# Dilated attention run in quarters of the heads beside the next products, with head gains folded into the turned copies and the rotation tables

## The chip, the cores and the metric

One core of one Trainium2 chip runs the whole program. The metric is the device time of one execution in microseconds (us), as the median of several runs. The engines are TensorE (PE, its weight load is PEld), VectorE (DVE), ScalarE (ACT), GpSimd (POOL) and SyncE (SP, which only issues the loads of weights). Each engine executes its own list of instructions strictly in order and waits on semaphores for the others.

## What is computed

Two blocks of two layers each over 256 tokens of width 1024, in float32. The change touches one sublayer, the dilated attention of layer 1 of the first block:

```python
def dilated_attention(h, cos, sin, w_in, q_gain, k_gain, w_out):
    B, S, _ = h.shape
    H, hd = DIL_HEADS, HEAD_DIM                      # 16 heads of 64
    proj = (h @ w_in).reshape(B, S, N_DIL_GROUPS, 3, H, hd)
    outs, lses = [], []
    for g, (window, dilation) in enumerate(DIL_CONFIGS):      # (128,1) (512,4) (2048,16)
        q = apply_rope(rms_norm(proj[:, :, g, 0], q_gain[g]), cos, sin)
        k = apply_rope(rms_norm(proj[:, :, g, 1], k_gain[g]), cos, sin)
        o, lse = dilated_group(q, k, proj[:, :, g, 2], window, dilation)
        outs.append(o)
        lses.append(lse)
    alpha = jax.nn.softmax(jnp.stack(lses, axis=0), axis=0)
    o = jnp.sum(alpha[..., None] * jnp.stack(outs, axis=0).astype(jnp.float32), axis=0).astype(h.dtype)
    return o.reshape(B, S, H * hd) @ w_out
```

`rms_norm` is taken over the 64 elements of a head, and `apply_rope` turns only the first 16 of them.

## The kernel before, in words

A planner (class `Plan`/`Program`) writes one list of steps; every engine's program then walks that list and emits its own part of each step, so the order of the list is the order on each engine. Weights are read in pieces of 1 MB (four chunks of 128 rows by 512 columns) into six raw buffers. For exact float32 products each piece is converted to a high part on ACT (`whi`, step `conv_hi`) and a low part on DVE (`wlo`, `conv_lo`), into three buffers; a conversion is planned when an earlier piece is taken, and waits for PE to have read the buffer. A product unit (`token`) uses two pieces: 24 matmuls of 512 columns each, high times high, high times low, low times high.

The dilated sublayer takes 18 units: for each half of the heads (8 heads) and each of three groups, q, then k, then v (`dil_in`). After a q or k unit a head norm runs: ACT squares the two result banks, DVE sums per head (`TENSOR_REDUCE dhs`), ACT takes the root, DVE takes the reciprocal, multiplies the banks by it (event `hn_mul`, which also frees the two banks), multiplies by the gain (`dgn`), does six small multiplies with the rotation table (`rope`) and an add (event `hn_out`). PE then turns the result (`head_turn`, eight transposes into banks D0 and D1) and ACT copies it out as `dqT` or `dkT`. In the code before, this turn is planned at the end of the following unit (`run_turns` in `token`).

When a half's nine units are done, `dil_attn` plans its attention in one block with no products between: ten steps, each two heads for one half of the queries. The parts of a step are the scores (PE), the mask and row minimum (DVE, `S,nm<-ps,dmask`, event `biased`), the exponentials (ACT, event `expd`), the reciprocal and its multiply (DVE, event `weighed`), the turn of the weights of the two heads (PE, `ps<-ident,S`), its copy (ACT, `PT`) and the product with v (PE, `ps<-PT,dv`). For even steps a head has 256 columns of scores, for odd ones 512. The second half's block is followed by the out product (`out_units`): four pieces, whose banks for the first two pieces are D0 to D3 before. The output of the first half is kept in `doT` and split into high and low parts just before the second block.

The older forgetting attention of layer 0 already runs its attention beside products: `beside` is a list of closures, and `run_beside` pops one after each part of a piece (`self.parts`).

## Time and profile before

| | us |
|---|---|
| median of 3 runs | 2218.18 (2216.0 to 2218.39) |
| profiled execution, its own time | 2219.53 |
| span of the profiled execution | 2218.2 |
| PE busy | 2140.0 (96%) |
| DVE busy | 1497.4 (68%) |
| ACT busy | 1082.5 (49%) |
| mean granted TensorE clock | 0.988 of full |

PE is the engine that sets the time: it is busy for 96% of the span, and the other engines matter where PE waits for them. A time inside the span is read from its start. The dilated sublayer's products begin at 793.96 and its out product ends at 1090.68.

### The profile page before, as it was taken

Reading aid. Unit: us, or ns where it says so; the run is one execution under the profiler, and the core shown is the slowest. Engines: PE = TensorE matmul, PEld = TensorE weight load, DVE = VectorE, ACT = ScalarE, POOL = GpSimd, SP = SyncE. Lnnn points to the kernel's source line nnn. Section 1 sums busy time; section 2 is a strip of 40 time slices with the busy share of each in tenths; the row PEclk is TensorE's granted clock in tenths of the full one; section 3 lists DMA queues with packets and bytes.
Section 4 is the critical chain, followed back from the end, with each engine's and each line's share of the span. In section 5 each row is a group of like instructions: output and inputs, shape, how many; then the busy total and the mean of one; then the engine's idle time right before and its main releaser. Section 6 shows DMA issues by size and latency. Waiting matters only on the chain.

```text
span 2218.2 us, 33120 instructions
## 1 busy us (share of the span) xinstructions
PE 2140.0 (96%) x14096; PEld 1889.0 (85%) x14096; DVE 1497.4 (68%) x1960; ACT 1082.5 (49%) x1217; POOL 156.6 (7%) x192
## 2 busy tenths in 40 slices
PE   7999998999999999899999999999999999999998
PEld 5998765998899878687799887897998878988996
DVE  4677676877777786576655455568786655677874
ACT  4443565543444354555544346644554457444652
POOL 0311110111011100000000011100000111000000
PEclk9999998999999999999999999999999999999999
DMA  9977662987787855244355564435655564446651
GB/s 347 307 267 263 249 244 86 302 279 271 249 273 257 288 210 182 88 171 152 115 191 189 190 226 169 171 124 166 217 178 194 194 211 153 136 152 209 190 176 53
DMA packets 262818, 448.61 MB, mean 202 GB/s; under 512 B 11616, under 2 KB 147104, under 8 KB 262416
## 3 DMA queue, kind: packets, MB, share of 16 engines
q1 hardware_dynamic: 243616, 376.64, 50.2%
q0 software_dynamic: 18768, 68.75, 8.8%
q8 instruction: 111, 1.82, 0.3%
q10 hardware_dynamic: 288, 1.11, 0.1%
q14 instruction: 35, 0.29, 0.0%
HBM read 445.40 MB, written 1.06 MB: 201 GB/s over the span
## 4 chain that ended last, share of the span: by engine, by line
PE 88%; ACT 5%; DVE 5%; issue 1%; DMA 0%; SPq 0%; ACTq 0%; DVEq 0%
PE ps L1522 86%; ACT whi L1747 2%; DVE wlo L1952 1%; PE ps L1713 1%; PE ps L1680 1%; ACT S L1747 1%; ACT L1747 1%; ACT xhi L1747 1%; ACT xs L1747 0%; DVE S L2100 0%; DMA raw<-in_mod_w 0%; PE ps L1670 0%; DVE nbuf L2060 0%; ACT PT L1747 0%; PE ps L1630 0%
## 5 line engine op out<-in xcount | busy, mean ns | idle before, releaser
L1952 DVE TENSOR_TENSOR wlo<-raw,whi 128x2048 fp32r<-128x2048 f32 (+1 forms) x339 | 767.2, 2271 | 349.8 <-ACT whi L1747 349.3
L1747 ACT ACTIVATE whi<-raw 128x2048 fp32r<-128x2048 f32 (+1 forms) x339 | 640.7, 1895 | 363.6 <-PE ps L1522 343.7
L1522 PE MATMUL ps<-xhi,whi 128*128 128x256 f32 x2632 | 649.8, 287 | 6.4 <-DVE wlo L1952 4.4
L1522 PE MATMUL ps<-xhi,wlo 128*128 128x256 f32 x2632 | 643.5, 284 | 0.0
L1522 PEld LDWEIGHTS ps<-xhi,whi 128*128 128x128 f32 x2632 | 507.9, 193 | 11.7 <-issue 7.2
L1522 PEld LDWEIGHTS ps<-xhi,wlo 128*128 128x128 f32 x2632 | 508.0, 193 | 2.3 <-issue 2.0
L1522 PE MATMUL ps<-xlo,whi 128*128 128x256 f32 x2632 | 344.3, 283 | 0.1
L1522 PEld LDWEIGHTS ps<-xlo,whi 128*128 128x128 f32 x2632 | 327.6, 192 | 0.5 <-DVE xlo L2066 0.3
L1522 PE MATMUL ps<-whi,xhi 128*128 128x512 f32 x736 | 296.7, 403 | 13.5 <-DVE wlo L1952 10.5
L1522 PE MATMUL ps<-wlo,xhi 128*128 128x512 f32 x736 | 290.4, 395 | 0.0
L1522 PE MATMUL ps<-whi,hhi 128*128 128x512 f32 x528 | 210.0, 398 | 0.0
L1522 PE MATMUL ps<-wlo,hhi 128*128 128x512 f32 x528 | 209.8, 397 | 0.0
L1522 PE MATMUL ps<-whi,hlo 128*128 128x512 f32 x528 | 207.9, 394 | 0.0
L1522 PE MATMUL ps<-whi,xlo 128*128 128x512 f32 x736 | 185.7, 391 | 0.0
L1522 PEld LDWEIGHTS ps<-whi,xhi 128*128 128x128 f32 x736 | 140.5, 191 | 48.4 <-issue 11.6
L1522 PEld LDWEIGHTS ps<-wlo,xhi 128*128 128x128 f32 x736 | 140.6, 191 | 27.8 <-issue 0.2
L1522 PEld LDWEIGHTS ps<-whi,xlo 128*128 128x128 f32 x736 | 139.3, 189 | 29.3
L1522 PEld LDWEIGHTS ps<-whi,hhi 128*128 128x128 f32 x528 | 99.2, 188 | 25.1 <-issue 0.7
L1522 PEld LDWEIGHTS ps<-whi,hlo 128*128 128x128 f32 x528 | 99.1, 188 | 23.5
L1522 PEld LDWEIGHTS ps<-wlo,hhi 128*128 128x128 f32 x528 | 99.2, 188 | 23.5 <-issue 0.7
L1747 ACT ACTIVATE e<-ps 128x512 f32<-128x512 f32 (+1 forms) x48 | 30.4, 634 | 172.4 <-PE ps L1522 172.3
L1747 ACT ACTIVATE hhi<-e 128x512 fp32r<-128x512 f32 x66 | 41.7, 632 | 114.0 <-DVE e L2254 71.2
(234 smaller groups left out, 1966.7 us busy)
## 6 DMA issues: line engine op xcount, KB each, us to landing
raw<-in_w_in SPq DMA_DIRECT2D x52, 1024.0 KB, 4.9
raw<-in_ffn_w_gate SPq DMA_DIRECT2D x88, 512.0 KB, 4.6
raw<-in_ffn_w_up SPq DMA_DIRECT2D x88, 512.0 KB, 6.0
raw<-in_ffn_w_down SPq DMA_DIRECT2D x44, 1024.0 KB, 5.0
raw<-in_w_up SPq DMA_DIRECT2D x88, 512.0 KB, 4.8
raw<-in_dil_w_in SPq DMA_DIRECT2D x36, 1024.0 KB, 5.1
xs<-in_mod_w POOLq DMA_DIRECT2D x54, 512.0 KB, 6.2
nbuf<-in_mod_w POOLq DMA_DIRECT2D x46, 512.0 KB, 5.2
```

The costliest lines, as they stand in the source:

```text
L1522: return nc.tensor.matmul(o, lhs, rhs, start=start, stop=stop, skip_group_check=True)
L1680: ins = nc.tensor.transpose(ps[:, D2, h * T + b * P:h * T + (b + 1) * P], w["S"][:, j, b * P:(b + 1) * P], ident[:, :])
L1713: ins = nc.tensor.transpose(ps[:, D0 + c // 2, (c % 2) * T + t * P:(c % 2) * T + (t + 1) * P], tms[s["name"]][:, t, c * P:(c + 1) * P], id ...
L1747: return nc.scalar.activation(o, i, func, **kw)
L1952: V.tensor_tensor(wlo[:, s["c"], 0:s["n"]], raw[:, s["slot"], 0:s["n"]], whi[:, s["c"], 0:s["n"]].bitcast(F32), ALU.subtract).then_inc(sem ...
```

## The change

The attention of the sublayer is made in quarters (4 heads, n = 0 to 3) and taken apart into smaller steps that are placed between halves of product pieces.

- Units: `dil_qk(n, g)` makes q and k of a quarter in one unit (256 columns each), `dil_values_in` makes v of a half. The order is qk 0, v 0, qk 1, qk 2, v 1, qk 3, each for the three groups.
- `self.parts` is two halves of a piece; after each half piece `run_beside` pops one entry. For quarters 0 to 2 the attention is 13 entries: per step p one with scores and exponentials of p and values of p-1, one with the reciprocal and its multiply (`weigh`), one with the turn. `None` entries (7, 0, 6, 0) delay it.
- `turns_early`: a head norm's turn is planned after the first piece of the following unit and no longer at its end.
- Quarter 3's attention (six entries, `last_step`) is placed beside the out product, whose units now use banks G0 to G3; the first two chunks of its second pieces are made early (`early=2`).
- The gain multiply of the head norm is gone for the dilated heads: the gains of the 48 unturned elements are the scale of ACT's copies `dqT` and `dkT` (`dgc`), those of the 16 turned ones are multiplied into the rotation tables once, on POOL (`dil_rope`, tile `drp`). The norm's work tile is now `nbuf`, and its rotation scratch `mrow`.

The diff, cut to its core:

```diff
+            if self.turns_early:
+                self.run_turns()
...
+    def dil_qk(self, n, g):
+
+        if g == 0:
+            self.at = self.dil_heads[n] = []
+        b0, b1, tok = self.token(self.need_x)
+        if (n, g) == (3, 2):
+            for c in range(4):
+                self.split_chunk(c, ("dil", 0), self.o_ready[c])
+        turn = self.head_norm(b0, b1, tok, "dil", g, ("dil", g, n % 2), [self.gain, self.late, self.rope_gain], self.dil_scored[n % 2])
+
+        def begin():
+            turn()
+            self.beside.extend([None] * (7, 0, 6, 0)[n] + self.dil_attention(n))
+
+        if (n, g) == (3, 2):
+            self.beside.extend([None] * 6 + [begin])
...
+        else:
+            self.turns.append(begin if g == 2 else turn)
...
+        def step(p, part):
+            if part == 0 and p < 4 * n + 4:
+                scores(p)
+                exps(p)
+            if part == 0 and p > 4 * n:
+                values(p - 1)
+            if part == 1:
+                weigh(p)
+            if part == 2:
+                turn(p)
+
+        def last_step(p):
+            if p < 16:
+                scores(p)
+            if p > 13:
+                values(p - 2)
+            if 12 < p < 17:
+                turn(p - 1)
+            if p < 16:
+                exps(p)
+                weigh(p)
...
+        pcs = self.last_two()
+        for kk in range(early):
+            for u in range(2):
+                self.token_step(pcs[u], need, src, base + u, base + 2 + u, 4, NC, (kk,), [])
+                self.run_beside()
         while self.beside:
             self.run_beside()
...
-                tail = self.out_units("x", self.need_x, lambda: Tail(self, "gate", "rms", 1, 1))
+                tail = self.out_units("x", self.need_x, lambda: Tail(self, "gate", "rms", i, 1), G0, True, 2 * i)
...
-                    V.tensor_tensor(tv, tv, gain.unsqueeze(1).to_broadcast([P, 16, 64]), ALU.mult).then_inc(sem["hn_out"])
...
+                        act(dq[:, :, :].rearrange("p c (t r i) -> p (c t) r i", t=2, r=2),
+                            ps[:, D0, :].rearrange("p (c i r) -> p c r i", c=4, r=2), ACT.Identity,
+                            scale=dil_gc[:, 0, g:g + 1]).then_inc(sem["head_kept"])
```

How this moves instructions is seen in three places. Line numbers are those of the kernel that the rows belong to. The first is DVE in the attention, before: the mask of two heads is followed at once by their reciprocals and multiplies (`ri<-rs` and `S<-S,ri`).

```order
L2092 ISA S,nm<-ps,dmask 128x256 [waits score]
L2092 ISA nm 128x1
L2092 ISA S,nm<-ps,dmask 128x256
L2092 ISA nm 128x1
L2097 RECIPROCAL ri<-rs 128x1 [waits expd]
L2100 TENSOR_SCALAR S<-S,ri 128x256 [waits weighed]
L2097 RECIPROCAL ri<-rs 128x1 [waits expd]
L2100 TENSOR_SCALAR S<-S,ri 128x256 [waits weighed]
```

In the change the same place for step 2 of quarter 0, after the first qk unit of quarter 1 (n = 1, g = 0). The rows left out are five of the six rotation multiplies and, after the last row, the second head's.

```order
L2169 ISA S,nm<-ps,dmask 128x256 [waits turned,score]
L2169 ISA nm 128x1
L2169 ISA S,nm<-ps,dmask 128x256 [waits turned]
L2169 ISA nm 128x1
L2190 TENSOR_REDUCE dhs<-nbuf 128x16 [waits hn_sq]
L2192 RECIPROCAL dhs<-dhs 128x16 [waits hn_sqrt]
L2195 TENSOR_TENSOR nbuf<-ps,dhs 128x1024 [waits head_turn,hn_rec]
L2206 TENSOR_TENSOR mrow<-nbuf,drp 128x8x16 [waits hn_mul]
...
L2213 TENSOR_TENSOR nbuf<-mrow 128x16x16 [waits ropa]
L2029 TENSOR_TENSOR wlo<-raw,whi 128x2048 [waits w_hi]
L2174 RECIPROCAL ri<-rs 128x1 [waits expd]
L2177 TENSOR_SCALAR S<-S,ri 128x256 [waits weighed]
```

Between the mask and the reciprocal there now stand that unit's whole head norm and the low part of a weight piece.

The second place is PE around the same step: scores (`dkT,dqT`), values of the step before (`PT,dv`), two half pieces of products (left out but for their last row), then the turn of the two heads' weights and the head norm's turn (`ident,nbuf`).

```order
L1588 MATMUL ps<-dkT,dqT 128x128 [waits biased,pt]
L1588 MATMUL ps<-dkT,dqT 128x128
L1588 MATMUL ps<-dkT,dqT 64x64 x8
L1588 MATMUL ps<-PT,dv 64x128 x4
L1588 MATMUL ps<-PT,dv 64x64 x8
...
L1588 MATMUL ps<-whi,xlo 128x512 x4
L1736 MATMUL ps<-ident,S 128x128 [waits weighed]
L1736 MATMUL ps<-ident,S 128x128
L1736 MATMUL ps<-ident,S 128x128 [waits biased,weighed]
L1736 MATMUL ps<-ident,S 128x128
L1780 MATMUL ps<-ident,nbuf 128x128 [waits biased,pt,hn_out]
L1780 MATMUL ps<-ident,nbuf 128x128 x7
```

The turn is two half pieces behind the scores, and waits for `weighed`, which DVE reaches only after the rows above.

The third place is PE where the last product unit (n = 3, g = 2) ends and the out product begins.

```order
L1588 MATMUL ps<-wlo,xhi 128x512
L1588 MATMUL ps<-whi,xlo 128x512 x4
L1588 MATMUL ps<-whi,xhi 128x512 [waits split_hi,w_lo,hn_mul]
L1588 MATMUL ps<-wlo,xhi 128x512
L1588 MATMUL ps<-whi,xhi 128x512
L1588 MATMUL ps<-wlo,xhi 128x512
L1588 MATMUL ps<-whi,xlo 128x512 [waits split_lo]
```

The out product's first matmul waits for `hn_mul`, the multiply of the last head norm: its banks G0 and G1 are those of the last unit. In the code before the last unit was a v unit and the block of attention stood in between.

On ACT, 56 table loads before are 68 after: the root of a head norm and the exponentials use different tables, and they now alternate.

## Rows read from the trace of the kernel before

**Rows 1.** The page: busy time, share of the span and instructions of each engine.
```profile
PE 2140.0 (96%) x14096; PEld 1889.0 (85%) x14096; DVE 1497.4 (68%) x1960; ACT 1082.5 (49%) x1217; POOL 156.6 (7%) x192
```
**Rows 2.** Busy time by stretch: A:B length, PE, PEld, DVE, ACT, POOL, clock, DMA share, GB/s.
```profile
898.96:931.42 32.46, 25.50 (x355) 18.69 (x353) 17.46 (x65) 22.23 (x55) 0.00 (x0) 0.89 0.17 62
931.42:1035.47 104.05, 104.05 (x483) 86.60 (x480) 72.11 (x84) 50.84 (x40) 0.00 (x0) 1.00 0.47 163
1035.47:1068.69 33.22, 24.95 (x354) 18.48 (x352) 19.73 (x72) 23.54 (x59) 0.00 (x0) 0.90 0.18 61
```
**Rows 3.** Busy time by stretch: one pair of attention steps, and the slow start.
```profile
904.70:910.20 5.50, 5.36 (x44) 4.02 (x44) 3.69 (x15) 2.91 (x8) 0.00 (x0) 0.54 0.00 1
913.20:919.40 6.20, 5.62 (x94) 4.16 (x88) 3.71 (x15) 4.47 (x13) 0.00 (x0) 1.00 0.00 0
```
**Rows 4.** Timeline of PE: one piece of products, then a head turn.
```profile
845.82 0.39 PE L1522 MATMUL ps<-whi,xhi 128*128 128x512 f32 x1
...
851.26 1.03 PE L1713 MATMUL ps<-ident,S 128*128 128x128 f32 x8
852.05 0.48 PE L1522 MATMUL ps<-whi,xhi 128*128 128x512 f32 x1
```
**Rows 5.** Timeline of ACT and DVE: one head norm (the rotation multiplies left out).
```profile
853.25 1.02 ACT L1747 ACTIVATE S<-ps 128x1024 f32<-128x1024 f32 x1
...
856.19 1.23 DVE L2119 TENSOR_TENSOR S<-ps,dhs 128x1024 f32<-128x1024 f32 x1
857.45 1.23 DVE L2121 TENSOR_TENSOR S<-S,dgn 128x1024 f32<-128x1024 f32 x1
...
859.78 0.43 DVE L2136 TENSOR_TENSOR S<-PT 128x256 f32<-128x256 f32 x1
```
**Rows 6.** Groups by line and shape, 899 to 932: xcount, busy us, mean ns.
```profile
L1747 ACT ACTIVATE S<-S,nm 128x512 f32<-128x512 f32 x8 | 5.7, 715 | 0.2 <-DVE nm L2092 0.2
L2092 DVE CUSTOM_DVE_ANT_0 S<-ps,dmask 128x512 f32<-128x512 f32 x8 | 5.2, 687 | 0.3 <-PE ps L1522 0.3
L1747 ACT ACTIVATE S<-S,nm 128x256 f32<-128x256 f32 x8 | 4.0, 501 | 0.0
L2100 DVE TENSOR_SCALAR S<-S,ri 128x512 f32<-128x512 f32 x8 | 3.9, 487 | 0.3
L1747 ACT ACTIVATION_READ_ACCUMULATOR S<-S,nm 128x1 f32 x16 | 3.1, 192 | 0.0
L2092 DVE CUSTOM_DVE_ANT_0 S<-ps,dmask 128x256 f32<-128x256 f32 x8 | 3.1, 420 | 1.8 <-PE ps L1522 1.8
L1747 ACT ACTIVATE PT<-ps 128x256 f32<-128x256 f32 x8 | 3.0, 377 | 0.6 <-PE ps L1670 0.6
L2100 DVE TENSOR_SCALAR S<-S,ri 128x256 f32<-128x256 f32 x8 | 2.8, 354 | 0.3
L2097 DVE RECIPROCAL ri<-rs 128x1 f32<-128x1 f32 x16 | 2.6, 164 | 9.8 <-ACT S L1747 9.8
```
**Rows 7.** Groups by line and shape, 832 to 900: the conversions of a weight piece.
```profile
L1952 DVE TENSOR_TENSOR wlo<-raw,whi 128x2048 fp32r<-128x2048 f32 x12 | 27.1, 2287 | 9.7 <-ACT whi L1747 9.7
L1747 ACT ACTIVATE whi<-raw 128x2048 fp32r<-128x2048 f32 x12 | 22.9, 1910 | 5.3 <-PE ps L1522 5.3
```
**Rows 8.** Timeline of PE after idle times; the idle time stands in brackets.
```profile
1042.66 1.18 PE L1670 MATMUL ps<-ident,S 128*128 128x128 f32 x4 [3.82 <-DVE S L2100]
...
1095.57 1.35 PE L1630 MATMUL ps<-ident,xs 128*128 128x128 f32 x8 [1.94 <-DVE xs L2029]
...
792.64 1.09 PE L1630 MATMUL ps<-ident,xs 128*128 128x128 f32 x8 [1.77 <-DVE xs L2029]
```
**Rows 9.** Timeline of ACT: the split of four kept chunks.
```profile
1038.77 1.33 ACT L1747 ACTIVATE xhi<-doT 128x256 fp32r<-128x256 f32 x4
```
**Rows 10.** Timeline of ACT: the switch to the root's table after the first block.
```profile
943.68 1.28 ACT L1747 ACT_TABLE_LOAD   x1
944.98 0.31 ACT L1747 ACTIVATE dhs<-dhs,epst 128x16 f32<-128x16 f32 x1
```

More of the change, by code:

```diff
@@ L199, in run_beside @@
     def run_beside(self):
-        if self.beside:
-            self.beside.pop(0)()
+        step = self.beside.pop(0) if self.beside else None
+        if step:
+            step()
     def next_pair(self):
@@ new lines, in scores, with biased @@
+    def scores(self, name, c, p, n, banks, ready):
+        tok = self.ev("pe", "score")
+        self.add("scores", name=name, c=c, qt=p % 2, kl=n, banks=banks, bank_free=[self.free[b] for b in banks], ready=ready)
+        return tok
+    def biased(self, name, j, n, bank, score, ready=None):
+        tok = self.ev("dve", "biased")
+        self.add("bias", name=name, j=j, n=n, bank=bank, score=score, s_free=self.s_free[j % 4], ready=ready)
+        self.free[bank] = self.bias_done = tok
+        return tok
@@ new lines, in exps, with weigh, values @@
+    def exps(self, name, j, n, after):
+        tok = self.ev("act", "expd")
+        self.add("exp", name=name, j=j, n=n, biased=after)
+        return tok
+    def weigh(self, name, j, n, after):
+        tr, td = self.ev("dve", "weighed"), self.ev("dve", "weighed")
+        self.add("weigh", name=name, j=j, n=n, expd=after, recip=tr)
+        return td
+    def values(self, name, c, hd, p, kl, pt, ready):
+        tok = self.ev("pe", "value")
+        self.add("values", name=name, hd=hd, qt=p % 2, kl=kl, bank=D3, bank_free=self.free[D3] if p % 2 == 0 else None, pt=pt, ready=ready)
+        self.pt_free[0] = self.pt_free[1] = tok
+        return tok
@@ L583, in turn_pair, with attention @@
+    def attention(self, name, klen, ready, emit, bias_ready=None, after=None):
+        rec = []
+        def scores(p):
+            n = klen(p % 2)
+            tok = self.scores(name, p // 2, p, n, (D0, D1), ready[:-1] if p == 0 else [])
+            for w in range(2):
+                rec.append([self.biased(name, 2 * p + w, n, D0 + w, tok, bias_ready(2 * (p // 2) + w) if bias_ready else None), n])
         def turn_pair(p):
@@ L591, in turn_pair @@
                 rec[j].append(te)
-        def values(p):
-            c, qt = p // 2, p % 2
-            bank = D3 if compact else G2 + c % 2
-            kl = rec[2 * p][2]
-            tok = self.ev("pe", "value")
-            self.add("values", name=name, p=p, kl=kl, bank=bank, bank_free=self.free[bank] if qt == 0 else None,
-                     pt=[rec[2 * p][3], rec[2 * p + 1][3]], ready=ready[-1])
-            self.pt_free[0] = self.pt_free[1] = tok
-            if qt == 1:
-                emit(c, bank, tok)
         def step_of(p):
@@ L664, in head_norm, with head_turn @@
         self.free[b0] = self.free[b1] = t4
-        out = t7 if turned else t5
-        self.turns.append(lambda: self.head_turn(name, out, dst, 1.0))
-    def head_turn(self, name, after, dst, scale):
+        at = self.at
+        return lambda: self.head_turn(name, out, dst, 1.0, at, gain_ready, dst_free)
+    def head_turn(self, name, after, dst, scale, at, gain_ready=(), dst_free=None):
         tk = self.ev("pe", "head_turn")
-        te = self.ev("act", "head_kept")
-        self.add("head_turn", name=name, after=after, dst=dst, scale=scale, bank_free=[self.free[D0], self.free[D1]], head_turn=tk)
-        self.free[D0] = self.free[D1] = te
+        te = [self.ev("act", "head_kept") for _ in range(2 if name == "dil" else 1)]
+        self.add("head_turn", name=name, after=after, dst=dst, scale=scale, bank_free=[self.free[D0], self.free[D1]], head_turn=tk,
+                 gain_ready=gain_ready, dst_free=dst_free)
+        self.free[D0], self.free[D1] = te[0], te[-1]
@@ L813, in fox_in @@
         if r < 2:
-            self.head_norm(b0, b1, tok, "fox", r, ("fox", "qk"[r], hh), gain_ready=[self.gain, self.late])
+            self.turns.append(self.head_norm(b0, b1, tok, "fox", r, ("fox", "qk"[r], hh), [self.gain, self.late]))
         else:
@@ L835, in dil_begin @@
         self.late = self.late_loads("dil_loads", 3)
+        self.parts, self.turns_early = (range(0, 2), range(2, 4)), True
+        self.o_ready = [None] * 6
+        self.dil_heads = {}
+        self.dil_scored = [None] * 2
+        self.dil_v, self.dil_valued = [], None
+        self.dil_keep = self.emit_keep(("dil", 0), self.o_ready)
+        self.dil_split = self.emit_split("dil", "x", 6, self.x_split)
     def dil_gain(self):
         self.gain = self.ev("dve", "gain")
-        self.add("dil_gain", late=self.late)
```

313 lines of the change are left out of this document (158 added, 155 removed).

## The prediction, made before the changed kernel ran

> **What bounds the kernel now.** The page comes first: PE is busy for 96% of the span [rows 1], so a change counts by the time in which PE waits or runs slowly. Next the busy time by stretch. In a stretch of products alone PE is busy for all of 104.05 us at a granted clock of 1.00, though DVE and ACT have only 72 and 51 us to do there. The two blocks of attention last 32.46 and 33.22 us with PE busy for about 25, part of it at a lower clock [rows 2]. Those two blocks are what the change can win. In the middle of a block two steps repeat every 6.2 us with 5.62 us of PE's work at full clock [rows 3]. Eight such pairs are 45.0 us, so of the 65.7 us in the blocks **20.7 us** are waits and slow clock. Were all attention covered by products, the time would fall by just that.
>
> The prices of the parts follow. A weight piece takes PE 5.44 us and a head turn with its aftermath about 0.9 [rows 4]. A head norm runs from the square's start at 853.25 to the end of `hn_mul` at 857.42, which is 4.17 us, and on to the end of its add at 860.21. Without the gain multiply of 1.23 that is 5.7 us from square to add [rows 5]. A pair of masks is 0.8 us (256 columns) or 1.35 (512), a first exponential with its read 0.65 or 0.85, a pair 1.15 or 1.65, a reciprocal and multiply 0.55 or 0.68 each, a pair of copies of turned weights 0.65 [rows 6]. A conversion is 1.9 us on ACT, then 2.25 on DVE at the pitch of a pair [rows 7].
>
> **The change, part by part.**
>
> *Removed:* both blocks, 20.7 us as above. The twelve gain multiplies, 14.7 us of DVE, shorten the norms as counted. Nothing else on PE goes away; its matmuls and turns stay as many.
>
> *Added at no cost:* twelve more table loads on ACT of 1.28 us. The load before a root lies beside the sum on DVE, and the root starts 1.30 us after the load did [rows 10]; the load before an exponential lies beside the scores. If that cover goes, each is 1.3 us on its chain. The Trainium skill, page ScalarE: Activation LUTs, section What ACT_TABLE_LOAD costs, has a switch cost 2.66 us with a drain of 1.38 behind the load. No drain shows in the row. By the page's 1.38, as an estimate, five chains would bring some 7 us more. Twenty-four more loads on SP, with half as long rows, in a stretch where the DMA engines are busy for 0.47 of the time [rows 2]: no cost, and if they came late, the conversions would. POOL's two table products need some us at the start, before the first norm's multiply; nothing.
>
> *(a) Early head turns.* A turn is now one piece, 5.44 us, behind its unit, and the norm needs 5.7 after the unit. Where no attention lies between (four units: n=0 and the last of n=1) PE waits 0.3 us each, **1.2 us**.
>
> *(b) A mask at a unit's end.* The main term. DVE works in order, and step 2 of quarter 0 has its mask before, and its reciprocal behind, the norm of the unit just ended. From the end of the scores: first mask and two exponentials 1.55, copy of an output 0.4, norm 5.7, low part 2.25, two reciprocals and multiplies 1.05, semaphores 0.3, in all 11.2 us until the second head may turn. PE has the values (1.05) and two half pieces (5.44) to do, and the first head's turn (0.3): 6.8. It waits about 4.2 us, and the head norm's turn then waits 0.4 for the copy that frees bank D0: 4.6. Before it, step 0's mask falls before a conversion: exponentials 1.55, 1.9, 2.25, weighing 1.1, less 5.44 and 0.3, is another 1.2. Quarter 2 has the same pattern: 2 x 5.8 = **11.6 us**.
>
> *(c) Quarter 1* is laid one half piece later. Its first norm ends, with a low part and both masks of step 5 behind it on DVE, 9.95 us after the unit; PE, with 5.44 of products, the turn, scores and values in 7.85, waits 2.1 for the bank, then 0.7 for step 5's weighing. The next norm holds up step 6's mask for 1.9. Step 7 is a case (b) with 512 columns: 2.35 + 5.7 + 2.25 + 1.35 and semaphores, less what PE has (0.6 + 5.44 + 0.65), 4.9 and 0.6 for the bank. Together **10.2 us**.
>
> *(d) The end.* The out product may not start before the last norm's `hn_mul`: four splits on ACT of 1.33 [rows 9], then 4.17 [rows 5], plus a semaphore: 5.6. Nothing else stands in PE's queue. Its seven chunks hide the rest of that norm. The six last steps have one chunk (1.36 us) between them, against a chain of mask, exponentials and weighing of 3 to 4 us with a conversion in the midst: I count 2.5 us at step 14's scores, 0.5 at step 15's turn and 0.7 at its values. Together **9.3 us**.
>
> *(e) Clock.* After 3.82 us idle PE is granted half speed for a while; after 1.94 too, after 1.77 not [rows 8]. Of the price: 904.7 to 910.2 is such a time, at 0.54 [rows 3], and does in 5.4 us what takes 3.4 at full clock, so 2.05 us. Four waits are clearly long enough: (b) twice, step 7 and the out product: **8.2 us**. Three near 2 us could add up to 6; with none the term is 0.
>
> The sum: 1.2 + 11.6 + 10.2 + 9.3 + 8.2 = 40.5 added, 20.7 removed, net **+19.8 us**. On the profiled execution's 2219.5 us that is 2239.3; the median of the runs shown is 1.35 us lower, so **2238.0 us**. Bounds: without term (e) 2229.8, with three more slow times 2244, a few us more if small switches cost more. The forecast's own range is 2229 to 2247.
>
> **Rivals.**
>
> *The waits of (b) and (c) do not come* (faster). The mechanism: reciprocal and multiply reach DVE within the 6.8 us that PE has to do, so the turns find their rows ready and all of quarters 0 to 2 is hidden. Then only (a), (d) and one slow time stay: 2218.2 - 20.7 + 1.2 + 9.3 + 2.05 = 2210. It decides at 11.2 against 6.8 us: 4.4 us would have to vanish from a chain of measured parts in an order that is fixed. For it: the stretch of products shows both engines with a third of their time free. Against: the order of rows on DVE. Chance 0.10.
>
> *The waits absorb one another* (no change). If PE's wait in one unit gives DVE and ACT the lead for the next, (b) and (c) could come to half, and the clock be lost twice: 1.2 + 10.9 + 9.3 + 4.1 - 20.7 = +5, and with (d) shorter about 2220. I followed the lead through in (c) and it was gone each time by the next norm. Chance 0.08.
>
> *The waits come, but not the slow clock* (slower, less): 2230, by the 1.77 us row. Chance 0.15.
>
> *The table switches cost time on the chain* (slower, more). If each root started a load's length (1.28 us) later than counted, five chains of (b) and (c) would be that much longer: 2238 + 6 = 2244. The gap of 1.30 us between load and root speaks against it [rows 10]. Chance 0.05. The drain in the page of the Trainium skill named above would act in this way.
>
> That the change does not do what it says can be left out: the order shows the attention between the pieces.
>
> **How the numbers follow.** The forecast has 0.62. Every case but the first two is slower by more than 0.2% (4.4 us, about what a measurement of this kernel can tell from no change): 0.82. No change 0.08, faster 0.10. The range from 2222 to 2248 leaves out the faster case, part of the second, and a few hundredths above.
>
> **What would show it.** In the changed profile: PE waiting about 4 us for `S` of DVE in two places, about 5 in a third, at turns of weights (`ident,S`); about 5.6 us before the first out product, released by DVE's `hn_mul`; waits of about 2 us at head turns in quarter 1; the clock near one half behind each long wait; the sublayer from 793.96 to 1090.68 longer by some 20 us, other stages unchanged. Wrong would be turns without waits, or a sublayer shorter than 290 us.

## The result, and the profile after

The changed kernel takes **2248.95 us** (median of 4 runs, 2245.12 to 2250.83) against 2218.05 for the kernel before (4 runs). The ratio is 1.0141, with a 95% interval of 1.0129 to 1.0154: slower by 31 us. The forecast was 2238 us in a range of 2222 to 2248, so the sign was right, the size too small by a third, and the time lies 1 us above the range.

The page's busy times of the changed kernel, which answer to [rows 1]:

```profile
PE 2144.9 (96%) x14096; PEld 1885.6 (84%) x14096; DVE 1483.7 (66%) x1948; ACT 1101.6 (49%) x1243; POOL 158.1 (7%) x194
```

DVE has 13.7 us less to do, about the twelve multiplies that went, ACT 19 more, and PE is as busy as before in its share: the page alone would not show what became slower. The busy times by stretch do (columns as in [rows 2]). First the changed kernel: all before the sublayer, the sublayer, the stretch from its last product to the next stage's first, and the rest.

```profile
0.00:789.32 789.32, 750.47 (x5029) 657.28 (x5029) 561.05 (x734) 360.08 (x413) 107.89 (x152) 0.99 0.77 262
789.32:1111.17 321.85, 291.28 (x1762) 229.65 (x1762) 187.05 (x319) 176.28 (x234) 2.57 (x5) 0.96 0.41 137
1111.17:1120.51 9.34, 4.57 (x34) 2.90 (x33) 4.90 (x12) 5.54 (x12) 0.00 (x0) 0.87 0.76 253
1120.51:2243.80 1123.29, 1098.54 (x7276) 995.78 (x7274) 730.67 (x885) 559.72 (x587) 47.62 (x38) 0.99 0.52 174
```

The same four stretches of the kernel before:

```profile
0.00:793.96 793.96, 757.71 (x5028) 664.13 (x5029) 561.14 (x734) 359.90 (x413) 107.64 (x152) 0.98 0.76 260
793.96:1090.68 296.72, 281.48 (x1762) 228.59 (x1762) 202.28 (x335) 159.90 (x211) 1.24 (x3) 0.98 0.42 149
1090.68:1096.96 6.28, 4.30 (x34) 2.26 (x33) 3.19 (x8) 3.01 (x9) 0.00 (x0) 0.94 0.63 208
1096.96:2218.20 1121.24, 1096.52 (x7274) 994.07 (x7274) 730.78 (x885) 559.70 (x587) 47.69 (x38) 0.99 0.52 175
```

The sublayer is 25.1 us longer, the stretch behind it 3.1, and the rest 2.1; the part before it is 4.6 shorter. To split a sublayer's length further, I take PE's idle time (length less busy time), the time that slow clock cost (busy time multiplied by one less the granted clock, summed over windows of 1 us), and what remains, PE's work at full clock:

| sublayer | length | idle | slow clock | work at full clock |
|---|---|---|---|---|
| before | 296.72 | 15.2 | 6.3 | 275.2 |
| changed | 321.85 | 30.6 | 11.9 | 279.4 |

Idle time and slow clock together rise by 21.0 us, where the forecast had 19.8. Work at full clock rises by 4.2 us although no matmul was added, and the stretch behind grows by 3.1: these two the forecast did not have. The part before the sublayer, in which both kernels do the same work (DVE x734, ACT x413 and POOL x152 in both rows), is discussed with the verdict.

Here are PE's waits of 0.25 us or more in the changed sublayer and at its end, in order of time (the idle time and its releaser in brackets; `ident,nbuf` is a head turn, `ident,S` a turn of attention weights; rows that repeat one shown are left out).

```profile
808.29 1.09 PE L1780 MATMUL ps<-ident,nbuf 128*128 128x128 f32 x8 [1.46 <-DVE nbuf L2213]
...
863.44 0.90 PE L1736 MATMUL ps<-ident,S 128*128 128x128 f32 x4 [0.48 <-DVE S L2177]
889.24 1.15 PE L1736 MATMUL ps<-ident,S 128*128 128x128 f32 x4 [3.51 <-DVE S L2177]
890.91 1.94 PE L1780 MATMUL ps<-ident,nbuf 128*128 128x128 f32 x8 [0.52 <-issue]
...
937.27 1.06 PE L1780 MATMUL ps<-ident,nbuf 128*128 128x128 f32 x8 [1.76 <-DVE nm L2169]
944.42 1.25 PE L1736 MATMUL ps<-ident,S 128*128 128x128 f32 x8 [0.62 <-DVE S L2177]
954.95 1.06 PE L1780 MATMUL ps<-ident,nbuf 128*128 128x128 f32 x8 [1.72 <-DVE nm L2169]
973.97 1.64 PE L1736 MATMUL ps<-ident,S 128*128 128x128 f32 x8 [4.51 <-DVE S L2177]
976.35 1.94 PE L1780 MATMUL ps<-ident,nbuf 128*128 128x128 f32 x8 [0.73 <-issue]
...
1068.35 0.80 PE L1588 MATMUL ps<-whi,xhi 128*128 128x512 f32 x1 [5.53 <-DVE nbuf L2195]
1090.28 0.41 PE L1736 MATMUL ps<-ident,S 128*128 128x128 f32 x2 [3.33 <-DVE nm L2169]
1104.34 1.12 PE L1588 MATMUL ps<-PT,dv 128*64 128x128 f32 x24 [0.78 <-ACT PT L1814]
1118.89 1.97 PE L1696 MATMUL ps<-ident,xs 128*128 128x128 f32 x8 [4.77 <-DVE xs L2106]
```

The last row is the wait that stood at 1.94 before (1095.57, [rows 8]). Of the others, all but one are in places that the prediction named. The one is the wait of 3.33 us: the prediction had 2.5 us at step 14's scores and 0.5 at step 15's turn, and PE waited at neither. It waited at the turn of step 12's second head, whose bank D0 comes free with step 13's mask, and on DVE that mask stood behind a low part:

```profile
1087.23 2.29 DVE L2029 TENSOR_TENSOR wlo<-raw,whi 128x2048 fp32r<-128x2048 f32 x1 [1.25 <-ACT whi L1814]
1089.44 0.68 DVE L2169 CUSTOM_DVE_ANT_0 S<-ps,dmask 128x512 f32<-128x512 f32 x1
```

DVE around the wait of 3.51 (the reciprocal, the rotation multiplies and the add left out):

```profile
879.42 0.42 DVE L2169 CUSTOM_DVE_ANT_0 S<-ps,dmask 128x256 f32<-128x256 f32 x1
...
881.86 1.22 DVE L2190 TENSOR_REDUCE dhs<-nbuf 128x16 f32<-128x1024 f32 x1 [2.00 <-ACT nbuf L1814]
...
883.76 1.23 DVE L2195 TENSOR_TENSOR nbuf<-ps,dhs 128x1024 f32<-128x1024 f32 x1
...
886.43 2.28 DVE L2029 TENSOR_TENSOR wlo<-raw,whi 128x2048 fp32r<-128x2048 f32 x1
888.63 0.16 DVE L2174 RECIPROCAL ri<-rs 128x1 f32<-128x1 f32 x1
```

ACT had finished both exponentials, with their reads, at 880.64. The reciprocal that PE waited for came 8.0 us later, behind 2.0 us in which DVE itself waited for the square, and behind the norm and the low part.

ACT in the same place, where the changed table is loaded beside DVE's sum:

```profile
881.84 1.28 ACT L1814 ACT_TABLE_LOAD   x1
883.13 0.31 ACT L1814 ACTIVATE dhs<-dhs,epst 128x16 f32<-128x16 f32 x1
```

The load ends with the sum (883.08) and the root starts 1.29 us after the load did: the switch costs nothing here, as the prediction had it.

### The profile page after: what moved, and what is told of

Same layout as the page of the kernel before. It is cut to its first block, busy times and chain, and to the rows that moved or that the text cites. A ratio compares the mean times of both kernels' runs of the same rounds, so it can differ in the third digit from the quotient of the medians.

```text
span 2243.8 us, 33163 instructions
## 1 busy us (share of the span) xinstructions
PE 2144.9 (96%) x14096; PEld 1885.6 (84%) x14096; DVE 1483.7 (66%) x1948; ACT 1101.6 (49%) x1243; POOL 158.1 (7%) x194
## 3 DMA queue, kind: packets, MB, share of 16 engines
HBM read 445.30 MB, written 1.06 MB: 199 GB/s over the span
## 4 chain that ended last, share of the span: by engine, by line
PE 80%; DVE 9%; ACT 6%; DMA 2%; issue 2%; SPq 0%; ACTq 0%; DVEq 0%
PE ps L1588 78%; DVE wlo L2029 3%; ACT whi L1814 2%; DMA xs<-in_mod_w 1%; DMA raw<-in_ffn_w_up 1%; PE ps L1780 1%; ACT L1814 1%; ACT S L1814 1%; DVE nbuf L2195 1%; PE ps L1746 1%; PE ps L1736 1%; DVE nbuf L2137 1%; ACT xhi L1814 1%; ACT xs L1814 0%; ACT nbuf L1814 0%
## 5 line engine op out<-in xcount | busy, mean ns | idle before, releaser
L1588 PE MATMUL ps<-whi,xhi 128*128 128x512 f32 x736 | 302.6, 411 | 19.1 <-DVE wlo L2029 10.5
L1588 PE MATMUL ps<-whi,xlo 128*128 128x512 f32 x736 | 194.3, 392 | 0.0
L1588 PEld LDWEIGHTS ps<-whi,hhi 128*128 128x128 f32 x528 | 99.2, 188 | 25.1 <-issue 0.7
```

Source lines behind the costliest of these rows:

```text
L1588: return nc.tensor.matmul(o, lhs, rhs, start=start, stop=stop, skip_group_check=True)
```

## The experiments

Twelve kernels were run, each against the kernel before on the same chip. They come in the order in which they ran. The kernel before took 2217.56 us beside the first four, 2217.34 beside the next four and 2219.34 beside the last four (16, 27 and 16 runs), so kernels of different groups are compared by their ratios to it and by their profiles. "The sublayer" is measured as in the table above.

### One step group moved: q0_shift

```diff
+            steps = self.dil_attention(n)
+            if n == 0:
+                steps = steps[:6] + [None] * 3 + steps[6:9] + [None] + steps[9:]
-            self.beside.extend([None] * (7, 0, 6, 0)[n] + self.dil_attention(n))
+            self.beside.extend([None] * (7, 0, 6, 0)[n] + steps)
```

> The changed kernel with one difference: in quarter 0 three empty entries stand ahead of step 2 and one ahead of step 3, so both masks are planned at the third half piece of a unit and their weighing at the fourth, ahead of the unit's head norm on VectorE; the last values still come before quarter 1 begins. Theory A (term (b): the wait comes from VectorE's order, mask before and reciprocal behind the norm): the waits of 3.51 and 0.52 us at step 2 of quarter 0 go, and with them the half-speed stretch behind them (some 2 us); head turns without attention near them cost 0.35 each as elsewhere. Quarter 2, left as it was, keeps its 3.50 and 0.52. About 6 us less than the change: 2243. Rival B (VectorE and ScalarE lack time in these units whatever the order): the wait moves to steps 2 and 3 at their new places with the same sum, 2249.

Measured: 2243.92 us (2240.74 to 2247.56, 4 runs), ratio 1.0113 (1.0097 to 1.0130). The sublayer is 315.40 us, 6.45 less than in the change. Between 870 and 935 one short wait is left, of 0.37 at a head turn; quarter 2, left as it was, still has its own:

```profile
888.73 1.09 PE L1783 MATMUL ps<-ident,nbuf 128*128 128x128 f32 x8 [0.37 <-DVE nbuf L2216]
...
1035.18 1.15 PE L1739 MATMUL ps<-ident,S 128*128 128x128 f32 x4 [3.50 <-DVE S L2180]
```

The same instructions at other half pieces don't wait. It is order, not load: rival B falls.

### Weighing planned behind the exponentials: weigh_first

```diff
             if part == 0 and p < 4 * n + 4:
                 scores(p)
                 exps(p)
+                weigh(p)
...
-            if part == 1:
-                weigh(p)
```

> The changed kernel with the reciprocals and multiplies of a step in quarters 0 to 2 planned right behind its exponentials (before any head norm that comes later), slots of scores, turns and values unchanged. Theory A: turns of weights no longer wait in (b) and at step 7 (3.51, 3.50, 4.51 and the clock behind them, 17 us together), but the norm that now stands behind two reciprocals and multiplies ends some 2 to 3 us later, so its head turn waits 1 to 2 us in place of the bank's 0.5 to 0.7; net 9 to 12 us less than the change, 2237 to 2240. Rival B (time is short in any order): the head turns then wait as long as the weights did, 2247 to 2250.

Measured: 2225.61 us (2222.60 to 2228.18, 6 runs), ratio 1.0030 (1.0019 to 1.0042), so 23 us less than the change, twice what was expected. The sublayer is 299.03 us, with 17.6 idle, 3.5 of slow clock and 277.9 of work. All waits at turns of weights in quarters 0 to 2 are gone. What had been expected in their place was mostly not paid:

```profile
890.33 1.06 PE L1779 MATMUL ps<-ident,nbuf 128*128 128x128 f32 x8 [0.58 <-DVE nbuf L2212]
...
935.78 1.06 PE L1779 MATMUL ps<-ident,nbuf 128*128 128x128 f32 x8 [1.78 <-DVE nm L2168]
...
968.75 1.09 PE L1779 MATMUL ps<-ident,nbuf 128*128 128x128 f32 x8 [0.84 <-DVE nbuf L2212]
```

The head turn at 890.33 waits 0.58, not 1 to 2. DVE shows why: the two weighings fill the time in which it stood waiting for the square (2.00 idle before, 0.63 now), so the norm is hardly later.

```profile
883.76 0.16 DVE L2173 RECIPROCAL ri<-rs 128x1 f32<-128x1 f32 x1 [0.32 <-ACT S L1813]
...
885.44 1.22 DVE L2189 TENSOR_REDUCE dhs<-nbuf 128x16 f32<-128x1024 f32 x1 [0.63 <-ACT nbuf L1813]
```

The idle time fell by 12.9 us and the slow clock by 8.4: three long waits had taken a slow stretch each, and with the waits all three went. The remaining 1.5 came off PE's work at full clock.

### The out product's banks exchanged: banks

```diff
-            b0, b1 = base + u, base + 2 + u
+            b0, b1 = (base + u, base + 2 + u) if not early else (base + 2 * (1 - u), base + 3 - 2 * u)
...
-        bank = pl.sum_banks + 2 * t + h
+        bank = pl.sum_banks + (2 * (1 - h) + t if pl.swapped else 2 * t + h)
```

> The changed kernel with the two pairs of banks of the out product exchanged: its first piece adds in G2 and G3 (free since the unit before), its second in G0 and G1, which the last head norm still reads when the out product starts. Term (d) and its clock: the 5.53 us before the first out product go and the half-speed stretch behind it too (some 2.5 us), 8 us less than the change, 2241; the conversions and the head turn of the last norm are covered. Rival: the splits of the first chunks (5.3 us on ScalarE, planned before the norm) hold the same matmul, and the wait stays at 4 to 5 us: 2248.

Measured: 2243.21 us (2242.42 to 2244.58, 4 runs), ratio 1.0110 (1.0096 to 1.0124), 5.7 less than the change; its sublayer is 6.8 us shorter. The wait at the first out product is now 0.66, for the split on ACT:

```profile
1068.29 0.47 PE L1590 MATMUL ps<-whi,xhi 128*128 128x512 f32 x1 [0.66 <-ACT xhi L1816]
```

So `hn_mul` was the releaser and 4.9 of the 5.53 us were its own; the splits, the rival, held the rest. The 8 us that had been expected did not come in full, because the slow clock of the sublayer fell only from 11.9 to 10.2 us.

### Early chunks alone, in the kernel before: before_early

```diff
         pcs = self.last_two()
+        for kk in range(early):
+            for u in range(2):
+                self.token_step(pcs[u], need, src, base + u, base + 2 + u, 4, NC, (kk,), [])
         tail = begin()
...
-            toks = [... range(4), [], (t,)) for u in range(2)]
+            toks = [... range(early, 4), [], (t,)) for u in range(2)]
...
-                tail = self.out_units(...)
+                tail = self.out_units(..., early=2)
```

> The kernel before with one part of the change alone: the first two chunks of the out product's last two pieces are made for both halves of the tokens before the tail, so that the last matmuls come 1.36 us apart per result bank and no longer 2.72; nothing else is moved. If the change's wait of 4.77 us (before: 1.94) at the turn behind the out product comes from this (the chain of gate, residual and statistics, about 5.8 us per token half, is no longer covered by products), this kernel is 2.8 to 3 us slower than before, some 2221, with the wait near 4.8 us. If that wait comes from the attention that runs late beside the out product, this kernel is as before, 2218, with 1.94.

Measured: 2221.55 us (2218.29 to 2224.00, 11 runs) against 2217.56 for the kernel before, ratio 1.0011 (1.0002 to 1.0020), which is 2.4 us (0.4 to 4.4), where the medians are 4.0 apart. The time alone says little, then; the profile says more. Its sublayer (296.18 us) is that of the kernel before, and the stretch behind it is 9.11 us, where before has 6.28 and the change 9.34:

```profile
1097.27 1.97 PE L1633 MATMUL ps<-ident,xs 128*128 128x128 f32 x8 [4.53 <-DVE xs L2032]
```

2.8 us, at the place and of the size that the change shows. It comes from the early chunks and not from the attention. Before, four steps of two matmul groups of 2.72 us each ended one result bank after the other, and the gate, residual and statistics of the first tokens ran beside them. With half of that work done ahead, the results come 1.36 us apart and the chain on DVE and ACT lies bare.

### Both edits together: wf_banks

Edit: the diffs of weigh_first and of banks.

> The two edits that each took a wait away, together: weighing planned behind the exponentials, and the out product's two pairs of banks exchanged. They touch different places (quarters 0 to 2; the start of the out product), so their gains should add: 23.3 and 5.7 us off the change's 2249 is 2220. Predicted 2219 to 2221, with PE's idle time in the sublayer at 12 to 13 us and no half-speed stretch but behind step 13's wait. Rival (one gain contains part of the other, by the clock): 2224.

Measured: 2218.12 us (2214.78 to 2220.82, 11 runs), ratio 1.0004 (0.9995 to 1.0013). The gains add, and come to 2 us more than the 2220 that the two give together. The sublayer is 292.16 us: idle 12.5, slow clock 1.5, work 278.1. It is shorter than the kernel before's 296.72, and the 3.1 us behind it give most of that back.

### The last conversion later: wf_banks_conv

```diff
-        pcs = self.last_two()
+        pcs = self.pieces[self.use:self.use + 2] if early else self.last_two()
...
+            if p == 15:
+                self.ensure(late=True)
             if p < 16:
                 scores(p)
...
                 weigh(p)
+            if p == 15:
+                self.convert_low()
```

> As wf_banks, and the conversion of the next stage's second piece, which stands ahead of step 13's mask on VectorE (2.25 us, between step 12's weighing and this mask) though no product needs it yet, is planned at step 15: its high part ahead of step 15's exponentials, its low part behind the last weighing, where VectorE is idle for 3 us. If that low part makes the 3.33 us wait at the turn of step 12's second head (its bank D0 is free only after step 13's mask), the wait goes to about 1 and the kernel is 2 to 4 us faster than wf_banks, some 2217. If the wait is the chain of step 12 itself, it stays and the time is as wf_banks.

Measured: 2215.48 us (2211.89 to 2218.37, 11 runs), ratio 0.9990 (0.9981 to 0.9998). The wait of 3.33 us is 0.55, and the sublayer 288.49 us. On DVE the low part stood between the weighing of step 12 and the mask of step 13. First wf_banks:

```profile
1062.15 2.29 DVE L2030 TENSOR_TENSOR wlo<-raw,whi 128x2048 fp32r<-128x2048 f32 x1 [1.25 <-ACT whi L1815]
1064.36 0.68 DVE L2170 CUSTOM_DVE_ANT_0 S<-ps,dmask 128x512 f32<-128x512 f32 x1
```

and wf_banks_conv:

```profile
1060.94 0.69 DVE L2174 CUSTOM_DVE_ANT_0 S<-ps,dmask 128x512 f32<-128x512 f32 x1 [0.67 <-PE ps L1593]
```

### Quarter 1 rearranged: combo

```diff
                 self.run_work(1)
+                if self.turns_early and ks[-1] == n - 1:
+                    self.run_turns()
                 self.run_beside()
-            if self.turns_early:
-                self.run_turns()
...
+            if n == 1:
+                steps = steps[:3] + [None] + steps[3:]
-            self.beside.extend([None] * (7, 0, 6, 0)[n] + self.dil_attention(n))
+            self.beside.extend([None] * (8, 1, 7, 0)[n] + steps)
```

> As wf_banks_conv, and in quarter 1 (a) the head turn is planned ahead of the attention entry of the same slot, so that it does not wait for the mask of that entry, which stands behind the head norm on VectorE, and (b) one empty entry stands ahead of step 5. PE's waits of 1.78, 1.75 and 0.84 at the head turns of quarter 1 should become one of about 1.7 (step 7, one half piece into its unit) and one of about 1 (scores behind the copy of the head turn): 1.6 us less than wf_banks_conv, 2215 to 2216. Rival: the waits only move, same time.

Measured: 2218.65 us (2215.43 to 2223.32, 11 runs), ratio 1.0006 (0.9997 to 1.0015): 3.2 us slower than wf_banks_conv, where 2215 to 2216 had been expected. The other numbers of empty entries (8, 1, 7) only make up for the head turn's being planned ahead of the slot's entry. Quarter 1 now has waits of 1.45 and 2.12 us, 0.8 less than its three before. The entry that I put into quarter 1 also moved quarter 2 by a half piece (its empty entries are counted from where quarter 1 ends), which I had overlooked, and there the same two waits appeared a second time (before: one of 0.57). Quarter 0 has 0.9 more as well.


```profile
1024.19 0.88 PE L1596 MATMUL ps<-dkT,dqT 64*128 64x128 f32 x20 [1.45 <-ACT dkT L1822]
1041.89 1.06 PE L1788 MATMUL ps<-ident,nbuf 128*128 128x128 f32 x8 [2.12 <-DVE nm L2177]
```

Scores right behind a head turn wait 1.45 us for ACT to copy their own banks out. One half piece of displacement is worth 3 us here.

### The gain multiply put back: gain_back

```diff
                     else:
+                        V.tensor_tensor(tv, tv, hs[:, 2, :].unsqueeze(2).to_broadcast([P, 16, 64]), ALU.mult).then_inc(sem["hn_out"])
+                        q.wait_ge(s["mid"])
```

> The changed kernel with a second multiply of 128x1024 in each of the dilated head norms, where the gain multiply was (it multiplies by the heads' factors once more, so the values differ; the duration, 1.23 us, and the place in the chain are those of the removed one). What the folded gain is worth beside this placing: four early head turns wait 1.23 longer each (4.9), steps 2, 7 and 10 wait 1.23 longer each (3.7), two head turns of quarter 1 too (2.5); the out product waits for the multiply before it and does not change. The early waits of 1.6 us stay without half-speed time, the one of 2.7 may have it (2). Some 11 to 14 us more than the change: 2260 to 2263. Rival: DVE has time to spare and the multiply is hidden, as it was before the change: 2249.

Measured: 2262.12 us (2258.80 to 2263.82, 4 runs), ratio 1.0201 (1.0187 to 1.0215): 13.2 us more than the change. The sublayer grows by 16.7 us, 10.3 of it idle time and 6.8 slow clock, since waits that had been short now are followed by a slow stretch as well:

```profile
948.28 1.94 PE L1781 MATMUL ps<-ident,nbuf 128*128 128x128 f32 x8 [3.03 <-DVE nm L2170]
...
989.96 1.97 PE L1737 MATMUL ps<-ident,S 128*128 128x128 f32 x8 [5.78 <-DVE S L2178]
```

Each is 1.27 above its counterpart in the change (1.76 and 4.51). Folding the gains was worth 13 us in this arrangement; the quarters without it would have been 2% slower than the kernel before (ratio 1.0187 to 1.0215).

### Low parts behind the masks: low_late

```diff
+            if self.turns_early:
+                self.ensure(ahead, late=True)
             pc = self.take(ahead)
...
                 self.run_work(1)
                 self.run_beside()
+                if self.turns_early and (ks[-1] == n - 1) == (k0 == 0):
+                    self.convert_low()
```

> As wf_banks_conv (2215.5, ratio 0.999), and in the dilated units the low part of a weight piece is planned later: behind the attention entry of the first piece's second half, and of the second piece's first half, in place of ahead of them. If the waits of 1.78 and 1.76 us at the head turns of quarter 1 come from VectorE having norm, low part (2.25) and only then the mask that frees bank D0, they go to 0 to 0.5 and the kernel takes 2212. If ScalarE or the norm itself holds them, or if the later low part is missed by the products, the time stays at 2215 or more.

Measured: 2213.05 us (2210.65 to 2215.63, 11 runs), ratio 0.9971 (0.9961 to 0.9980). The sublayer is 285.29 us, 3.2 shorter than in wf_banks_conv, with 7.4 idle and no slow clock at all; 1.0 of the 3.2 is slow clock that wf_banks_conv's profile had at the start of its sublayer, behind the wait ahead of it. Of the two waits, 1.76 is gone and 1.78 is 0.92, more than the 0 to 0.5 expected. DVE in wf_banks_conv, where the norm ends at 931.32:

```profile
931.24 2.29 DVE L2034 TENSOR_TENSOR wlo<-raw,whi 128x2048 fp32r<-128x2048 f32 x1
933.45 0.68 DVE L2174 CUSTOM_DVE_ANT_0 S<-ps,dmask 128x512 f32<-128x512 f32 x1
```

and in low_late, PE and DVE at the same place:

```profile
932.50 1.30 PE L1597 MATMUL ps<-dkT,dqT 64*128 64x256 f32 x20
933.87 0.69 DVE L2178 CUSTOM_DVE_ANT_0 S<-ps,dmask 128x512 f32<-128x512 f32 x1 [0.94 <-PE ps L1597]
935.32 1.06 PE L1789 MATMUL ps<-ident,nbuf 128*128 128x128 f32 x8 [0.92 <-DVE nm L2178]
```

The low part held the mask, and with it the bank, for 0.9 us of the 1.78. The other 0.92 has another cause: DVE now stands idle for 0.94 us ahead of the mask and takes it up as soon as the scores are there. The two masks take 1.3 us, and PE has only the values (0.67 us) between these scores and the head turn.

### An earlier last turn, one early chunk: begin_early

```diff
-            self.beside.extend([None] * 6 + [begin])
+            self.beside.extend([None] * 4 + [begin])
...
-                tail = self.out_units(..., G0, True, 2 * i)
+                tail = self.out_units(..., G0, True, i)
```

> As wf_banks_conv, with the last head turn two chunks earlier in the out product (the norm's add ends at 1051.4 there and the turn comes at 1054.8) and only one chunk of the second pieces made early in place of two, so that the last matmuls come 2.04 us apart. The tail behind the out product (9.37 us from the last product to the next stage's first) should fall by about 2, and the last steps' attention should have the same product slots; the two low parts (4.49 us) that now stand ahead of step 12's mask may cost 1 to 2. Predicted 2213 to 2215.5; over 2216 if the low parts cost more than the tail gives.

Measured: 2212.30 us (2207.53 to 2213.39, 6 runs), ratio 0.9962 (0.9946 to 0.9978). The stretch behind the sublayer falls from 9.37 to 7.32 us, as expected. The sublayer itself is 289.96, 1.5 longer than in wf_banks_conv: 0.45 of it is a wait at step 12's scores, the low parts ahead of the mask, and 0.7 is slow clock, which fell at another place (behind a wait of 1.77 us that had none in the profile of wf_banks_conv). Sublayer and stretch together are thus only 0.6 us shorter (297.28 against 297.86), while the ratio fell from 0.9990 to 0.9962, some 6 us. Most of that lies outside the part that was edited, and no run here explains it.

### low_late and begin_early together: all_in

Edit: the diffs of low_late and begin_early on wf_banks_conv.

> Both of the two edits above on wf_banks_conv: if they are independent, the sum of their gains, about 2210 to 2212, some 0.3% faster than the kernel before.

Measured: **2210.18 us** (2208.59 to 2212.78, 5 runs), ratio 0.9962 (0.9950 to 0.9975): 0.4% faster than the kernel before and, by the two ratios, 1.8% faster than the change. The ratio is that of begin_early, and its interval overlaps low_late's, so the times don't show that the gains add. The profiles speak for it: sublayer and stretch are 292.98 us together, against 294.63 in low_late, 297.28 in begin_early, 297.86 in wf_banks_conv and 303.00 before. The two stretches of its profile, to be read against 296.72 and 6.28 of before:

```profile
793.54:1079.25 285.71, 277.99 (x1763) 222.33 (x1763) 187.97 (x323) 177.98 (x237) 2.57 (x5) 1.00 0.47 154
1079.25:1086.52 7.27, 4.56 (x33) 2.85 (x33) 3.77 (x9) 3.61 (x9) 0.00 (x0) 0.90 0.73 223
```

### Leaving a run of products more often: before_split

```diff
+        split = name == "dil" and dst[1:] != ("k", 2)
+        self.add("head_turn", cs=range(2 if split else 4), last=not split, ...)
+        if split:
+            self.beside.append(lambda: self.add("head_turn", cs=range(2, 4), last=True, ...))
```

> The kernel before, with ten of the twelve dilated head turns cut in two: the first four transposes at the end of a unit as before, the last four behind the following unit's first piece. Same instructions, nothing waits (the heads are needed much later); PE leaves a run of products ten times more. If leaving a run and coming back costs PE 0.1 to 0.2 us, as half pieces of 2.90 us beside attention against 2.73 in a long run suggest, PE's work at full clock in the sublayer rises from 275.2 us by 1 to 2. If the longer half pieces come from ScalarE's and VectorE's traffic, it stays at 275.2.

Measured: 2239.68 us (2237.43 to 2243.29, 4 runs), ratio 1.0095 (1.0081 to 1.0110). "Nothing waits" was wrong. The square of the next head norm writes the tile that the delayed transposes read, so ACT started it only behind them:

```profile
818.98 1.03 ACT L1752 ACTIVATE S<-ps 128x1024 f32<-128x1024 f32 x1 [9.87 <-PE ps L1717]
```

and PE then waited for the norm, and once more for a low part behind it, 3.1 to 3.3 us in each of four places, and 1.5 in two more. The time of this kernel says nothing on the question, then. Its split does, weakly: PE's work at full clock is 277.65 us against 275.20, 2.4 for ten more interruptions. Since waits seem to add to that figure too (weigh_first lost 1.5 us of it with its waits), I take the bound from there: 26 more interruptions than before cost 2.7 us without long waits, 0.10 each, and up to 0.25 by before_split.

## Why the prediction was wrong, point by point

By its own terms, against the profiled execution of the change:

| term | forecast | measured |
|---|---|---|
| removed: waits and slow clock of the two blocks | 20.7 | 21.5 |
| (a) early head turns | 1.2 | 2.5 |
| (b) quarters 0 and 2 | 11.6 | 9.0 |
| (c) quarter 1 | 10.2 | 9.3 |
| (d) the out product's start and the last steps | 9.3 | 9.6 |
| (e) slow clock | 8.2 | 11.9 |
| PE leaving runs of products | 0 | 4.2 |
| the stretch behind the out product | 0 | 3.1 |

The measured waits are sums of the rows above: (b) is 0.48 + 3.51 + 0.52 twice, (c) 1.76 + 0.62 + 1.72 + 4.51 + 0.73, (d) 5.53 + 3.33 + 0.78.

**Right:** the mechanism, and its places but one. The walk along DVE's order gave 32.3 us of waits, and 30.5 came. Removing the causes one by one removed the waits one by one: q0_shift, weigh_first, banks, wf_banks_conv and low_late each took away the wait, low_late a part of it, that had been ascribed to the order that they change. In (a) the four waits of 0.3 were 0.34 to 0.35 in three cases and 1.46 in the first. There DVE was late: it was still at a low part that began at 801.42 when the square was done, and its sum began 1.86 us after the square did, against 1.06 at the second head turn (815.95 and 814.89). That is 0.8 of the extra 1.1. In (b), the gap of 0.4 assumed after step 2's wait was 0.52, and the 4.2 was 3.51: from the end of the scores (878.94) to the second weighing (889.64) it was 10.7 us where 11.2 were counted, and the two half pieces took 5.74 in place of 5.44. Step 0's 1.2 was 0.48; the parts listed for it add up to 1.06.

**Right in size by luck, part of (d):** the 5.6 us at the out product's start was 5.53 and came as forecast. For the last steps 3.7 us had been forecast at three waits and 4.1 came at two, but 3.3 of it at a turn that the prediction had not named, as the rows in the section on the result show. That step 13's mask frees the bank of step 12's second head is not in the prediction's walk.

**Mis-sized, term (e):** 2.05 us for each slow stretch and four of them. There were five, also one behind the 3.33 us wait in (d), and they cost 1.5, 3.1, 3.1, 2.6 and 1.7 us. These are busy time by one less the clock; the first and the third, in the changed kernel:

```profile
889.24:893.50 4.26, 3.74 (x16) 2.99 (x17) 0.37 (x2) 1.38 (x4) 0.00 (x0) 0.60 0.74 246
...
1036.29:1043.50 7.21, 6.69 (x22) 5.35 (x23) 0.84 (x3) 4.31 (x6) 0.00 (x0) 0.54 0.45 148
```

The step that failed was to price the slow stretch of the kernel before by a window that ended at 910.2 [rows 3], while the clock stayed low until 912 (busy times of the kernel before):

```profile
904.70:912.00 7.30, 7.16 (x60) 5.16 (x64) 4.62 (x19) 4.23 (x12) 0.00 (x0) 0.53 0.00 1
```

7.16 us by 0.47: that stretch cost 3.4. Even the shorter window gives 2.5 and not 2.05 (5.36 us by 0.46); the prediction's "what takes 3.4 at full clock" stands in no row.

**Failed, "nothing else on PE goes away; its matmuls and turns stay as many":** true of their number, not of their time. A half piece of products between two attention entries takes 2.90 us, as here from 875.22 to the scores at 878.12, and a run without interruption gives 2.72 for it (half of 5.44):

```profile
875.22 0.48 PE L1588 MATMUL ps<-whi,xhi 128*128 128x512 f32 x1
...
878.12 0.88 PE L1588 MATMUL ps<-dkT,dqT 64*128 64x128 f32 x20
```

The prediction used 5.44 per piece throughout. In all, PE's work at full clock grows by 4.2 us in the change and by 2.7 to 2.9 in the kernels without the long waits. The direct test was spoiled by its own waits, so the amount for one interruption stays between 0.10 and 0.25 us. The trace speaks for the interruption itself and against traffic of ACT and DVE, which one would expect to slow the matmuls in the middle as well: in this half piece the second matmul starts 0.31 us after the first, where 0.23 is usual in a run, and the last four take 0.99 us up to the scores, where they take 0.91 inside a run (881.94 to 882.85); the seven between keep their 0.23.

**Failed, "other stages unchanged":** the early chunks were counted as cover for the attention in (d), and not as cover taken from the chain behind the last matmul. before_early shows 2.8 us for that alone.

**What each step is worth.** The forecast of 19.8 us and the table's net of 28.1 us (49.6 less 21.5) differ by 8.3. The waits came 1.8 lower than forecast and the removed part 0.8 higher, both on the fast side; against them stand 3.7 more of slow clock, 4.2 for the interruptions and 3.1 for the stretch behind the out product. The time lay 1 us above the range, less than any one of these three.

**From the profile to the median.** The sublayer with the stretch behind it is 28.2 us longer. The profiled execution is only 25.6 us longer: its part before the sublayer had 5.2 us of slow clock where the kernel before had 12.7, and 2.6 us more idle time, and the part behind had 2.2 us more slow clock. It was also the fastest of its four runs; their median is 3.8 us above it, and the measured difference is 31. How often the clock falls behind the same wait of some 2 us varies from one execution to the next: the part before the sublayer alone had between 5.2 and 12.7 us of slow clock over the profiles of this study. This is 0.3% of the time, and no term of the forecast stood for it.

**Of the rivals,** "the waits of (b) and (c) do not come" and "the waits absorb one another" fell by the waits above, and "the waits come, but not the slow clock" by the slow stretches. "The table switches cost time on the chain" fell too: the root starts 1.29 us after its load, with the sum beside it. DVE waits 0.40 us for the root behind that load (883.48) and 0.38 where there is none (805.20). The drain behind a table load of which the Trainium skill tells (ScalarE: Activation LUTs, What ACT_TABLE_LOAD costs) shows in no row here; the trace does not agree with it.

What stays open is the last 0.3 us of the first head turn's wait, and how the 4.2 us of PE's work divide between interruptions and restarts after long waits. Neither was tried further.

## What to carry to other kernels

Work put beside an engine's main stream is placed on every in-order engine at once, so write down for each of them what stands between the two halves of a chain (here mask and reciprocal): the load average said that DVE had a third of its time free, and the order made PE wait 30 us all the same, where the blocks had made it wait 15. Plan the second half directly behind the first; it filled a gap that existed anyway, and this one edit of three lines gave back 23 of the 31 us. When work is taken ahead to cover one chain, ask which chain it covered until then, and price an interruption of the main stream even if nothing waits.

## What the runs showed that was not expected

- DVE stood idle for 2.00 us ahead of the norm's sum. With two reciprocals and multiplies put there the head turn waited 0.58 us in all, where 1 to 2 had been expected.
- What a slow stretch costs does not follow from the wait's length: behind 3.5 us of idle time it was 1.5 us in one case (889.24) and 3.1 in another (1036.29), which is nearly the wait once more. Removing three long waits in weigh_first saved 12.9 us of idle time and 8.4 of slow clock.
- Waits of 1.8 us at head turns were sometimes followed by a slow stretch and sometimes not: at quarter 1's 1.77 us wait in begin_early (935.30) the head turn took 1.81 us, and behind the same wait in the change (937.27) it took 1.06. The wait of 1.77 us ahead of the sublayer, which stands without slow clock in [rows 8], had it in wf_banks_conv: the turn behind it (791.10) took 1.92 us and not 1.09.
